# Two heads' stick-breaking scores made together on the halves of the matmul array

## Chip, cores and metric

One core of one Trainium2 chip. The metric is the device time of the kernel in microseconds, the median of several executions.

## What is computed

Two transformer blocks one behind the other, at 512 tokens and width 1024, in fp32. The change is in the first block's stick-breaking attention, 8 heads of 64:

```python
z = einsum('bhqd,bhkd->bhqk', q, k) * scale            # scores
strict = key_idx < q_idx
log_one_minus = where(strict, log_sigmoid(-z), 0)
suffix = cumsum(log_one_minus, reverse=True) - log_one_minus
w = where(strict, exp(log_sigmoid(z) + suffix), 0)
out = einsum('bhqk,bhkd->bhqd', w, v)
```

The query, key and value projections come before it; other projections of the same normalised input (latent ranks, gates) don't depend on it.

## The kernel before

The program is written engine by engine, with semaphores; each engine runs its own list in order. Weights come in chunks through three `raw` buffers; ScalarE copies a chunk into a rounded high part `whi`, VectorE subtracts it and gets `wlo`, each in four buffers. A projection tile is `project`: for 8 blocks of the inner dimension, three matmuls (low x high, high x low, high x high) of 512 columns into one PSUM bank, 24 in all. `bank(b)` waits until what was in bank b has been read (`free[b]`).

For the queries, ScalarE copies each head's 64 rows out of PSUM into a tile of its own (`qp[:, h, :]`), on rows 0 to 63 for even heads and 64 to 127 for odd ones; GpSimd fills the other 64 rows with zeros. Keys of two heads share a tile (`kp[:, h // 2, :]`). So a head's scores are a product over all 128 rows.

The attention of 8 heads is a loop over four pairs `pr`, with h = 2 pr. For one head:

- TensorE, `sb_qk`: transposed scores of four key blocks (512, 384, 128 and 256 query columns, the causal part only), each with a mask added by a small bf16 matmul. They lie in three banks, 0 to 2 for even heads and 3 to 5 for odd ones.
- VectorE, `sb_pre` (L1814): min(score, 40) into `sp`; ScalarE, `sb_pre` (L1313): exp, then ln(1 + x).
- VectorE, `sb_pre2` (L1822): maximum with the scores. ScalarE, `sb_pre2` (L1320): rounded copy `sph`; before it writes, it waits for SBSUF(h - 1), the suffix matmuls of the head before, which read the same single buffer. Low part `spl` by VectorE (last 256 columns, also in `sb_pre2`, waiting for the rounded copy) and by GpSimd (`sb_low`, 896 columns).
- TensorE, `sb_suffix`: suffix sums as products with triangular and all-ones tiles, added onto the scores. ScalarE, `sb_weights`: exp into `sp`.
- TensorE, `sb_pv`, once a pair: product with the values, head h into rows 0 to 63 of bank 6 and head h+1 into rows 64 to 127. VectorE copies it out (OA, L1846).

Between these steps every engine calls `next(fa)`, its share of one "filler": on TensorE a `project` (cq, ckv, kr, sz, mz, ga in turn) into bank 7 (three of the ga tiles go elsewhere), on ScalarE the conversion of a coming chunk, on VectorE the low part of that chunk, in some of the early fillers also a reduction over a chunk of `w_ada` (L1684), and then the copy of the filler's result out of its bank. The fillers are called equally often on all three engines, but in each engine's own order. Before the change, of one pair:

```
TensorE  sb_qk(h+1) | F1 | sb_suffix(h) | F2 | sb_qk(h+2) | F3 | sb_suffix(h+1) | F4 | sb_pv | F5
ScalarE  F1 | weights(h) | pre(h+1) | F2 | pre2(h+1) | F3 | weights(h+1) | F4 | pre(h+2) | F5 | pre2(h+2)
VectorE  F1 | pre(h+1) | F2 | pre2(h+1) | F3 | F4 | OA | pre(h+2) | F5 | pre2(h+2)
```

Ahead of the loop stand TensorE sb_qk(0), F0; ScalarE and VectorE pre(0), pre2(0), F0. In pair 2 ScalarE has eight silu activations between F5 and pre2.

Of the kernel before, what the change touches and what calls it, by code (L numbers as in the profile page):

```python
# [11 lines left out]
ALU = mybir.AluOpType  # L12
# [3 lines left out]
S = 512  # L16
# [86 lines left out]
BK = [0, 1, 2, 1]  # L103
# [3 lines left out]
KB_ORDER = (0, 1, 3, 2)  # L107
# [64 lines left out]
def build(nc, w_all, cst_d, rc_d, gc_d, rm_d, vec_d, x_d, c_d, pos_d, ada_d, p_d, out_d):  # L172
# [13 lines left out]
    with top:  # L186
# [3 lines left out]
        def sig(n, keys=(0,), step=1):  # L190
            return Sig(sem(n), keys, step)

        def sb(stack, name, shape, dt=F32):
            return stack.enter_context(nc.sbuf_tensor(name, shape, dt))

        PB = [top.enter_context(nc.psum_tensor(f"pb{i}", [128, 512], F32)) for i in range(8)]
# [23 lines left out]
        zs = sb(one, "zs", [128, 8, S])  # L220
# [15 lines left out]
            rn = sb(pre, "rn", [128, S])  # L236
            rk = sb(pre, "rk", [128, S])
        with ExitStack() as s1:
            qp = sb(s1, "qp", [128, 8, S])
            kp = sb(s1, "kp", [128, 4, S])  # L240
            sbv = sb(s1, "sbv", [128, 4, S])
            sp = sb(s1, "sp", [128, 2, 1280])
            sph = sb(s1, "sph", [128, 1280], F32R)
            spl = sb(s1, "spl", [128, 1280], F32R)
# [64 lines left out]
        identB, mcB, msB, mgB = (bcst[:, i, :] for i in range(4))  # L309
# [41 lines left out]
        def sb_out(h, kb):  # L351
            return PB[3 * (h % 2) + BK[kb]][:, BO[kb]:BO[kb] + LEN[kb]]
# [38 lines left out]
        MODS = sig("dve_mods", range(NB))  # L391
        ZPLE = sig("act_zple", range(8))

        QZERO = sig("pool_qzero", (0, 1))
        QPE, KPE, SBV = sig("act_qp", range(8)), sig("dve_kp", range(4)), sig("act_sbv", range(4))
        SBQK, SBMIN, SBLN, SBMAX, SBHI, SBLO0, SBLO1, SBSUF = (
            sig(n, range(8)) for n in ("pe_sbqk", "dve_sbmin", "act_sbln", "dve_sbmax", "act_sbhi", "pool_sblo",
                                       "dve_sblo", "pe_sbsuf"))
# [42 lines left out]
        def proj(name, idx=0, q=0):  # L441
            return PROJ((name, idx, q))
# [58 lines left out]
        def pool_program(e):  # L501
            G = Queue(e)
# [7 lines left out]
                e.tensor_tensor(dst, buf[64:96, 0, :], buf[64:96, 1, :], ALU.add).then_inc(ROPED.sem, 1)  # L510

            def sb_low(h):
                G.wait_ge(*QZERO(1))
                G.wait_ge(*SBHI(h))
                if h > 1:
                    G.wait_ge(*ROPED("kr"))
                if h:
                    G.wait_ge(*SBSUF(h - 1))
                e.tensor_tensor(spl[:, 0:896], sp[:, h % 2, 0:896], fr(sph[:, 0:896]), ALU.subtract).then_inc(SBLO0.sem, 1)
# [26 lines left out]
            G.wait_ge(*GPS.tick())  # L546
            e.tensor_scalar(ang[:, :], ang[:, :], lim, -lim, ALU.min, ALU.max).then_inc(ANG.sem, 1)

            G.wait_ge(*ROPE())
            G.wait_ge(*proj("pp", 1, 3))  # L550
            for r in range(2):
                if r:
                    G.wait_ge(*QZERO(0))
                e.memset(qp[64 - 64 * r:128 - 64 * r, :, :].rearrange("p (m r) n -> p m r n", r=2)[:, :, r, :], 0.0
                         ).then_inc(QZERO.sem, 1)
            for h in range(8):
                sb_low(h)
                if h == 1:
# [41 lines left out]
        def tensor_program(e):  # L600
            T = Queue(e)
            free = [[] for _ in range(8)]

            def mm(out, lhs, rhs, start, stop):
                return e.matmul(out, lhs, rhs, start=start, stop=stop, skip_group_check=True)  # L605

            def bank(b):

                for s, v in free[b]:
                    T.wait_ge(s, v)  # L610
# [98 lines left out]

            project_group([("sbq", i, 128, i) for i in range(4)], h1)  # L710
            for m in range(4):
                free[m] = [QPE(2 * m + 1)]
            for m in range(4):
                project("sbk", m, 128, 4 + m, h1)
                free[4 + m] = [KPE(m)]
# [30 lines left out]
                    free[b] = [GA67(m)]  # L746
                yield

            def sb_qk(h):
                T.wait_ge(*QPE(h))  # L750
                T.wait_ge(*QZERO(h % 2))
                T.wait_ge(*KPE(h // 2))
                T.wait_ge(*CONST())
                for kb in KB_ORDER:
                    out = sb_out(h, kb)
                    bank(3 * (h % 2) + BK[kb])
                    mm(out, kp[:, h // 2, 128 * kb:128 * kb + 128], qp[:, h, 128 * kb:512], kb != 3, False)
                    t = mm(out[:, 0:128], identB, msB, False, False)
                t.then_inc(SBQK.sem, 1)

            def sb_suffix(h):
                i = h % 2
                T.wait_ge(*SBMAX(h))
                for kb in range(4):
                    mm(sb_out(h, kb)[:, 128 * (3 - kb):128 * (4 - kb)], cb(O_TRI if kb == 3 else O_NONES),
                       sp[:, i, 896:1024], False, False)
                T.wait_ge(*SBLO0(h))
                T.wait_ge(*SBLO1(h))
                for kb in range(3):
                    for jb in range(kb, 3):  # L770
                        o = 128 * (jb - kb)
                        for src in (sph, spl):
                            t = mm(sb_out(h, kb)[:, o:o + LEN[jb]], triR if jb == kb else nonesR,
                                   src[:, SO[jb]:SO[jb] + LEN[jb]], False, False)
                t.then_inc(SBSUF.sem, 1)
                for b in range(3):
                    free[3 * i + b] = [SBW((h, b))]
# [15 lines left out]
            next(fa)  # L793
            for pr in range(4):
                h = 2 * pr
                sb_qk(h + 1)
                next(fa)
                sb_suffix(h)
                next(fa)
                if pr < 3:  # L800
                    sb_qk(h + 2)
                next(fa)
                sb_suffix(h + 1)
                next(fa)
                sb_pv(pr)
                if pr < 3:
                    next(fa)
            next(fa)

# [385 lines left out]
        def scalar_program(e):  # L1195
# [3 lines left out]
            def copy(out, in_, **kw):  # L1199
                return e.activation(out, in_, ACT.Copy, **kw)  # L1200
# [67 lines left out]
            A.wait_ge(*TRIG("cos"))  # L1268
            for m in range(4):
                A.wait_ge(*proj("sbq", m))  # L1270
                for r in range(2):
                    copy(qp[64 * r:64 * r + 64, 2 * m + r, :], PB[m][64 * r:64 * r + 64, :], scale=0.125
                         ).then_inc(QPE.sem, 1)
            for m in range(4):
                conv("sbk", m)
            for c in range(4):
# [36 lines left out]
            def sb_pre(h):  # L1313
                x = sp[:, h % 2, :]
                A.wait_ge(*SBMIN(h))
                e.activation(x, x, ACT.Exp).then_inc(ACS.sem, 1)
                A.wait_ge(*ACS.tick())
                e.activation(x, x, ACT.Ln, bias=one_c).then_inc(SBLN.sem, 1)

            def sb_pre2(h):  # L1320
                A.wait_ge(*SBMAX(h))
                if h:
                    A.wait_ge(*SBSUF(h - 1))
                copy(sph[:, :], sp[:, h % 2, :]).then_inc(SBHI.sem, 1)
# [7 lines left out]

            fa = filler_a()
            sb_pre(0)
            sb_pre2(0)
            next(fa)
            for pr in range(4):
                h = 2 * pr
                next(fa)
                sb_weights(h)  # L1340
                sb_pre(h + 1)
                next(fa)
                sb_pre2(h + 1)
                next(fa)
                sb_weights(h + 1)
                next(fa)
                if pr < 3:
                    sb_pre(h + 2)
                    next(fa)
                    if pr == 2:  # L1350
                        e.preload_act_table_set(SILU)
                        for m in range(8):
                            A.wait_ge(*ZE(m))
                            e.activation(zs[:, m, :], zs[:, m, :], ACT.Silu).then_inc(SIL.sem, 1)
                        e.preload_act_table_set(EXPLN)
                    sb_pre2(h + 2)
            next(fa)

            A.wait_ge(*ZA(3))
# [308 lines left out]
        def vector_program(e):  # L1668
# [3 lines left out]
            def tt(out, a, b, op):  # L1672
                return e.tensor_tensor(out, a, b, op)  # L1673
# [140 lines left out]
            def sb_pre(h):  # L1814
                V.wait_ge(*SBQK(h))
                if h > 1:
                    V.wait_ge(*SBPV(h // 2 - 1))
                for b, n in THIRDS:
                    t = e.tensor_scalar(sp[:, h % 2, 512 * b:512 * b + n], PB[3 * (h % 2) + b][:, 0:n], 40.0, None, ALU.min)
                t.then_inc(SBMIN.sem, 1)  # L1820
# [11 lines left out]

            fa = filler_a()
            sb_pre(0)
            sb_pre2(0)
            next(fa)
            for pr in range(4):
                h = 2 * pr
                next(fa)
                sb_pre(h + 1)  # L1840
                next(fa)
                sb_pre2(h + 1)
                next(fa)
                next(fa)
                V.wait_ge(*SBPV(pr))
                e.tensor_copy(qp[:, h, :], PB[6][:, :]).then_inc(OA.sem, 1)  # L1846
                if pr < 3:
                    sb_pre(h + 2)
                    next(fa)
                    sb_pre2(h + 2)  # L1850
            for m in range(4):
                V.wait_ge(*SIL(m))
                V.wait_ge(*OA(m))
                tt(zs[:, m, :], zs[:, m, :], qp[:, 2 * m, :], ALU.mult).then_inc(ZA.sem, 1)
            next(fa)

            for k in range(5):
# [553 lines left out]
```

## Time and profile before

| | |
|---|---|
| median of 3 runs | 1385.64 us (1383.92 to 1389.07) |
| profiled execution, its time | 1384.75 us |
| its span | 1382.9 us |
| busy: PE, weight loads, DVE, ACT, POOL | 1283.2, 1004.9, 704.0, 499.5, 101.1 us |
| chain that ended last: PE, DVE, ACT | 76%, 13%, 7% |

PE is TensorE's matmuls, PEld its weight loads, DVE VectorE, ACT ScalarE, POOL GpSimd. A row of the timeline gives the start in us from the span's start, the length, engine, line, operation, tiles written and read, shape and count; a bracket gives the idle time of that engine before it and what ended it. L605 is the matmul helper, which all of TensorE's projections and scores go through. Ends of matmuls are modelled: from one start to the next is the better measure. An fp32 matmul of the program stands as two passes.

### The profile page before, as it was taken

The page shows a single profiled execution, that of the slowest core. Times are in us where ns is not written, and L with a number is a line of the kernel's source. Part 1 is how long each engine was busy: PE and PEld are TensorE (multiplying, and loading weights), DVE is VectorE, ACT ScalarE, POOL GpSimd, SP SyncE. Part 2 cuts the span into 40 slices and gives each one's busy share as a digit, 9 for nine tenths or more (in the row PEclk, how much of TensorE's full clock was granted, in tenths as well). Part 3 has the DMA queues.
Part 4 walks back from the last instruction along what each step waited for, and adds up shares of the span by engine and source line. Part 5 has one row for each costly group of instructions (what it writes and reads, how often), then busy time and mean ns, then how long its engine had stood idle before and what let it go on. Part 6 is the DMA issues. An engine that isn't in the chain of part 4 may idle for free.

```text
span 1382.9 us, 14956 instructions
## 1 busy us (share of the span) xinstructions
PE 1283.2 (93%) x6048; PEld 1004.9 (73%) x6048; DVE 704.0 (51%) x1070; ACT 499.5 (36%) x793; POOL 101.1 (7%) x81
## 2 busy tenths in 40 slices
PE   2799999999998998999999898898999999999985
PEld 1577767776775776777776798786888888888864
DVE  3852574467556566536765675445333333332346
ACT  3451443443534343324456302223322222221233
POOL 7310111013000000000000300100000000000000
PEclk8799999999999999999999999999999999999998
DMA  7722332122121332221112000021322232333212
GB/s 283 274 77 76 103 122 77 62 69 88 46 61 46 97 128 94 84 84 61 46 51 72 16 1 1 31 75 51 118 92 91 94 102 94 114 110 100 93 48 85
DMA packets 35222, 118.16 MB, mean 85 GB/s; under 512 B 4001, under 2 KB 4257, under 8 KB 35153
## 3 DMA queue, kind: packets, MB, share of 16 engines
q1 hardware_dynamic: 33824, 112.68, 24.6%
q0 software_dynamic: 1328, 4.52, 1.1%
q8 instruction: 48, 0.79, 0.2%
q14 instruction: 22, 0.17, 0.0%
HBM read 112.99 MB, written 4.19 MB: 85 GB/s over the span
## 4 chain that ended last, share of the span: by engine, by line
PE 76%; DVE 13%; ACT 7%; issue 3%; DMA 1%; POOL 1%; DVEq 0%; SPq 0%; ACTq 0%
PE pb L605 73%; DVE wlo L1673 2%; DVE junk L1684 1%; ACT whi L1200 1%; DVE gq L1676 1%; PE pb L703 1%; ACT fP L1389 1%; DVE xT L1673 1%; PE pb L860 1%; DMA xT<-x_d 1%; DVE fP L1892 1%; DVE hlo L1673 1%; ACT mP L1389 1%; PE pb L687 1%; DVE mnm L1896 0%
## 5 line engine op out<-in xcount | busy, mean ns | idle before, releaser
L605 PE MATMUL pb<-hhi,wlo 128*128 128x512 f32 x1048 | 418.2, 399 | 17.6 <-ACT hhi L1200 9.8
L605 PE MATMUL pb<-hhi,whi 128*128 128x512 f32 x1048 | 417.2, 398 | 0.0
L605 PE MATMUL pb<-hlo,whi 128*128 128x512 f32 x1048 | 404.6, 403 | 11.9 <-DVE xT L1676 3.6
L1673 DVE TENSOR_TENSOR wlo<-raw,whi 128x1024 fp32r<-128x1024 f32 (+1 forms) x178 | 222.5, 1258 | 226.0 <-ACT whi L1200 225.8
L605 PEld LDWEIGHTS pb<-hhi,wlo 128*128 128x128 f32 x1048 | 198.1, 189 | 70.8 <-ACT hhi L1200 12.8
L605 PEld LDWEIGHTS pb<-hlo,whi 128*128 128x128 f32 x1048 | 198.8, 190 | 65.9 <-DVE wlo L1673 10.9
L605 PEld LDWEIGHTS pb<-hhi,whi 128*128 128x128 f32 x1048 | 198.4, 189 | 47.3
L1200 ACT ACTIVATE whi<-raw 128x1024 fp32r<-128x1024 f32 (+1 forms) x178 | 181.2, 1034 | 85.2 <-PE pb L605 85.1
L605 PE MATMUL pb<-alo,whi 128*128 128x512 f32 x176 | 69.6, 396 | 0.0
L605 PE MATMUL pb<-ahi,wlo 128*128 128x512 f32 x176 | 69.6, 396 | 0.0
L605 PE MATMUL pb<-ahi,whi 128*128 128x512 f32 x176 | 69.6, 395 | 0.0
L1200 ACT ACTIVATE ahi<-tmpf 128x512 fp32r<-128x512 f32 x22 | 13.9, 632 | 99.3 <-DVE tmpf L1673 99.3
L1673 DVE TENSOR_TENSOR tmpf<-tmpf,pb 128x512 f32<-128x512 f32 x22 | 15.1, 686 | 57.4 <-PE pb L605 57.4
L1605 ACT ACTIVATE sq<-xT 128x512 f32<-128x512 f32 x21 | 13.3, 632 | 84.8 <-DVE xT L1673 84.8
L1673 DVE TENSOR_TENSOR xT<-xT,pb 128x512 f32<-128x512 f32 x16 | 10.9, 686 | 55.2 <-PE pb L605 55.2
L605 PEld LDWEIGHTS pb<-ahi,wlo 128*128 128x128 f32 x176 | 33.1, 188 | 8.0
L605 PEld LDWEIGHTS pb<-ahi,whi 128*128 128x128 f32 x176 | 33.1, 188 | 8.0
L605 PEld LDWEIGHTS pb<-alo,whi 128*128 128x128 f32 x176 | 33.1, 188 | 8.0
L1632 ACT ACTIVATE tmpf<-pb 128x512 f32<-128x512 f32 x22 | 13.2, 599 | 61.9 <-PE pb L605 61.9
L1673 DVE TENSOR_TENSOR ssq<-ssq,sq 128x512 f32<-128x512 f32 x35 | 23.6, 691 | 21.7 <-ACT sq L1605 13.6
L1673 DVE TENSOR_TENSOR hlo<-tmpf,hhi 128x512 fp32r<-128x512 f32 x32 | 22.1, 691 | 21.5 <-ACT hhi L1200 21.5
L1200 ACT ACTIVATE hhi<-tmpf 128x512 fp32r<-128x512 f32 x32 | 20.2, 631 | 34.1 <-DVE tmpf L1676 33.9
(321 smaller groups left out, 1722.6 us busy)
## 6 DMA issues: line engine op xcount, KB each, us to landing
raw<-w_all SPq DMA_DIRECT2D x173, 512.0 KB, 3.5
adab<-ada_d SPq DMA_DIRECT2D x16, 512.0 KB, 9.2
raw<-w_all SPq DMA_DIRECT2D x10, 384.0 KB, 3.0
xT<-x_d SPq DMA_DIRECT2D x8, 256.0 KB, 8.6
ple_scratch<-zs SPq DMA_DIRECT2D x8, 256.0 KB, 2.3
xT<-x_d POOLq DMA_DIRECT2D x8, 256.0 KB, 3.0
out_d<-xT SPq DMA_DIRECT2D x8, 256.0 KB, 2.3
plr<-ple_scratch POOLq DMA_DIRECT2D x4, 256.0 KB, 3.6
```

What stands on the lines that cost most here:

```text
L605: return e.matmul(out, lhs, rhs, start=start, stop=stop, skip_group_check=True)
L687: t = e.matmul(PB[b][:, :], ones, src, start=True, stop=more is None)
L703: e.matmul(PB[7][:, :], ones, sq[:, b % 2, :], start=b == 0, stop=b == 7).then_inc(XSS.sem, 1)
L860: t = e.transpose(PB[b][:, o + 128 * (qi - kb):o + 128 * (qi - kb) + 128], P[:, PO[qi] + 128 * kb:PO[qi] + 128 * kb + 128], ident)
L1200: return e.activation(out, in_, ACT.Copy, **kw)
L1389: t = e.activation(d, src, ACT.Exp, bias=nm[:, i, qi:qi + 1], accum_out=rs[:, i, qi:qi + 1])
L1605: e.activation((sq[:, 1 - m % 2, :]) if m else ssq[:, :], xT[:, m, :], ACT.Square).then_inc(SQ.sem, 1)
L1632: e.activation(tmpf[:, j % 2, :], PB[2 * (j % 4)][:, :], ACT.Silu).then_inc(SG.sem, 1)
L1673: return e.tensor_tensor(out, a, b, op)
L1676: return e.scalar_tensor_tensor(out, a, s, b, op0, op1)
L1684: e.tensor_tensor_reduce(out=junk[:, :], in0=w, in1=cbt[:, :], scale=1.0, scalar=0.0, op0=ALU.mult, op1=ALU.add, accum_out=mod[:, at:at + ...
L1892: t = e.tensor_tensor_reduce(out=P[:, PO[qi]:PO[qi] + QN[qi]], in0=src, in1=cbt2[:, i, 0:QN[qi]], scale=1.0, scalar=-3.0e38, op0=ALU.add, ...
```

## The change

- `qp` has one tile for two heads: ScalarE copies all 128 rows at once. The zero fills on GpSimd and their waits are gone.
- `sb_qk(pr)` makes the scores of both heads of a pair: for each key block a matmul on rows 0 to 63 for head h and one on rows 64 to 127 for head h+1, in different banks; then the masks of head h, and those of head h+1.
- The orders of the three engines change with it:

```
TensorE  F1 | sb_suffix(h) | F2 | sb_suffix(h+1) | F3 | F4 | sb_pv | sb_qk(pair + 1) | F5
ScalarE  pre2(h+1) | F1 | weights(h) | F2 | weights(h+1) | F3 | F4 | pre(h+2) | pre(h+3) | pre2(h+2) | F5
VectorE  pre2(h+1) | F1 | F2 | F3 | F4 | OA | pre(h+2) | pre(h+3) | pre2(h+2) | F5
```

Ahead of the loop: TensorE sb_qk(pair 0), F0; ScalarE and VectorE pre(0), pre(1), pre2(0), F0. The silu block comes after F5 of pair 2.

```diff
-            qp = sb(s1, "qp", [128, 8, S])
+            qp = sb(s1, "qp", [128, 4, S])
...
-            G.wait_ge(*ROPE())
-            G.wait_ge(*proj("pp", 1, 3))
-            for r in range(2):
-                if r:
-                    G.wait_ge(*QZERO(0))
-                e.memset(qp[64 - 64 * r:128 - 64 * r, :, :].rearrange("p (m r) n -> p m r n", r=2)[:, :, r, :], 0.0
-                         ).then_inc(QZERO.sem, 1)
...
-            def sb_qk(h):
-                T.wait_ge(*QPE(h))
-                T.wait_ge(*QZERO(h % 2))
-                T.wait_ge(*KPE(h // 2))
+            def sb_qk(pr):
+
+                T.wait_ge(*QPE(pr))
+                T.wait_ge(*KPE(pr))
                 T.wait_ge(*CONST())
                 for kb in KB_ORDER:
-                    out = sb_out(h, kb)
-                    bank(3 * (h % 2) + BK[kb])
-                    mm(out, kp[:, h // 2, 128 * kb:128 * kb + 128], qp[:, h, 128 * kb:512], kb != 3, False)
-                    t = mm(out[:, 0:128], identB, msB, False, False)
-                t.then_inc(SBQK.sem, 1)
+                    for r in range(2):
+                        bank(3 * r + BK[kb])
+                        rows = slice(64 * r, 64 * r + 64)
+                        mm(sb_out(r, kb), kp[rows, pr, 128 * kb:128 * kb + 128], qp[rows, pr, 128 * kb:512], kb != 3, False)
+                for r in range(2):
+                    for kb in KB_ORDER:
+                        t = mm(sb_out(r, kb)[:, 0:128], identB, msB, False, False)
+                    t.then_inc(SBQK.sem, 1)
...
             for pr in range(4):
                 h = 2 * pr
-                sb_qk(h + 1)
                 next(fa)
                 sb_suffix(h)
                 next(fa)
-                if pr < 3:
-                    sb_qk(h + 2)
+                sb_suffix(h + 1)
                 next(fa)
-                sb_suffix(h + 1)
                 next(fa)
                 sb_pv(pr)
                 if pr < 3:
+                    sb_qk(pr + 1)
                     next(fa)
...
             sb_pre(0)
+            sb_pre(1)
             sb_pre2(0)
             next(fa)
             for pr in range(4):
                 h = 2 * pr
-                next(fa)
-                sb_pre(h + 1)
-                next(fa)
                 sb_pre2(h + 1)
                 next(fa)
                 next(fa)
+                next(fa)
+                next(fa)
                 V.wait_ge(*SBPV(pr))
-                e.tensor_copy(qp[:, h, :], PB[6][:, :]).then_inc(OA.sem, 1)
+                e.tensor_copy(qp[:, pr, :], PB[6][:, :]).then_inc(OA.sem, 1)
                 if pr < 3:
                     sb_pre(h + 2)
+                    sb_pre(h + 3)
+                    sb_pre2(h + 2)
                     next(fa)
-                    sb_pre2(h + 2)
```

## Rows read from the trace of the kernel before

**Rows 1.** The page, busy time of each engine (share of the span) and instructions
```profile
PE 1283.2 (93%) x6048; PEld 1004.9 (73%) x6048; DVE 704.0 (51%) x1070; ACT 499.5 (36%) x793; POOL 101.1 (7%) x81
```

**Rows 2.** Windows, pair end to pair end: busy PE, PEld, DVE, ACT, POOL; clock; DMA
```profile
178.09:221.70 43.61, 42.26 (x205) 31.71 (x203) 26.67 (x38) 17.45 (x20) 6.04 (x3) 1.00 0.36 121
...
262.93:303.70 40.77, 39.11 (x191) 30.54 (x189) 19.44 (x25) 23.75 (x29) 4.66 (x2) 1.00 0.17 55
sum 173.74, PE 167.39 PEld 127.90 DVE 93.43 ACT 77.64 POOL 20.03; mean PE 41.85 PEld 31.98 DVE 23.36 ACT 19.41 POOL 5.01
```

**Rows 3.** Timeline of PE, every row of the stage with a gap before it
```profile
144.21 0.47 PE L605 MATMUL pb<-hlo,whi 128*128 128x512 f32 x1 [3.34 <-DVE gbt L1784]
...
197.06 0.47 PE L605 MATMUL pb<-hlo,whi 128*128 128x512 f32 x1 [1.35 <-DVE zs L1803]
...
279.55 0.50 PE L605 MATMUL pb<-sph,rcst 128*128 128x512 f32 x1 [1.66 <-POOL spl L519]
```

**Rows 4.** Timeline of PE: scores of head 0, the filler behind them, next scores
```profile
129.96 1.02 PE L605 MATMUL pb<-qp,kp 128*128 128x512 f32 x2
...
130.82 0.22 PE L605 MATMUL pb<-bcst 128*128 128x128 bf16 x1
...
132.48 0.48 PE L605 MATMUL pb<-hlo,whi 128*128 128x512 f32 x1
...
138.16 1.02 PE L605 MATMUL pb<-qp,kp 128*128 128x512 f32 x2
```

**Rows 5.** Timeline of PE: values of pair 0 and the filler behind them
```profile
175.78 2.37 PE L605 MATMUL pb<-sp,sbv 128*64 128x512 f32 x16
178.09 0.48 PE L605 MATMUL pb<-hlo,whi 128*96 128x512 f32 x1
```

**Rows 6.** Timeline of DVE: chain of head 0 and the filler's copy
```profile
132.71 1.62 DVE L1819 TENSOR_SCALAR sp<-pb 128x512 f32<-128x512 f32 x3 [15.51 <-PE pb L605]
137.06 1.62 DVE L1673 TENSOR_TENSOR sp<-pb,sp 128x512 f32<-128x512 f32 x3 [2.74 <-ACT sp L1318]
...
140.97 2.49 DVE L1673 TENSOR_TENSOR wlo<-raw,whi 128x1024 fp32r<-128x1024 f32 x1 [0.52 <-ACT whi L1200]
143.38 0.68 DVE L1784 COPY gbt<-pb 128x512 f32<-128x512 f32 x1
```

**Rows 7.** Timeline of ACT: the same chain, second half
```profile
135.67 1.37 ACT L1318 ACTIVATE sp<-sp,epsc 128x1280 f32<-128x1280 f32 x1
138.72 1.27 ACT L1200 ACTIVATE sph<-sp 128x1280 fp32r<-128x1280 f32 x1 [1.69 <-DVE sp L1673]
139.90 1.04 ACT L1200 ACTIVATE whi<-raw 128x1024 fp32r<-128x1024 f32 x1
```

**Rows 8.** Timeline of DVE, pair 0: low part of head 1 to the next copy
```profile
163.90 0.42 DVE L1673 TENSOR_TENSOR spl<-sp,sph 128x256 fp32r<-128x256 f32 x1 [1.34 <-ACT sph L1200]
...
168.46 0.68 DVE L1784 COPY gbt<-pb 128x512 f32<-128x512 f32 x1
```

**Rows 9.** Timeline of DVE, pair 1: low part to the copy of sz0
```profile
190.40 0.43 DVE L1673 TENSOR_TENSOR spl<-sp,sph 128x256 fp32r<-128x256 f32 x1 [1.34 <-ACT sph L1200]
...
196.24 0.68 DVE L1803 COPY zs<-pb 128x512 f32<-128x512 f32 x1
```

**Rows 10.** Timeline of DVE, pair 2: low part to the next copy
```profile
232.41 0.42 DVE L1673 TENSOR_TENSOR spl<-sp,sph 128x256 fp32r<-128x256 f32 x1 [1.34 <-ACT sph L1200]
...
235.82 0.68 DVE L1803 COPY zs<-pb 128x512 f32<-128x512 f32 x1
```

**Rows 11.** A gap of a later stage, and windows (columns as rows 2) after gaps
```profile
431.39 0.50 PE L605 MATMUL pb<-hlo,whi 128*128 128x512 f32 x1 [3.27 <-DVE xT L1676]
144.20:148.00 3.80, 3.79 (x16) 3.09 (x17) 2.22 (x3) 1.48 (x2) 0.00 (x0) 1.00 0.76 219
431.40:435.00 3.60, 3.60 (x11) 2.90 (x12) 2.34 (x4) 0.64 (x1) 0.00 (x0) 0.70 0.55 148
435.00:439.00 4.00, 4.00 (x22) 2.79 (x20) 1.77 (x3) 0.60 (x1) 0.00 (x0) 0.84 0.00 0
```

More of the change, by code:

```diff
@@ L392, in build @@
         ZPLE = sig("act_zple", range(8))
-        QZERO = sig("pool_qzero", (0, 1))
-        QPE, KPE, SBV = sig("act_qp", range(8)), sig("dve_kp", range(4)), sig("act_sbv", range(4))
+        QPE, KPE, SBV = sig("act_qp", range(4)), sig("dve_kp", range(4)), sig("act_sbv", range(4))
         SBQK, SBMIN, SBLN, SBMAX, SBHI, SBLO0, SBLO1, SBSUF = (
@@ L512, in sb_low @@
             def sb_low(h):
-                G.wait_ge(*QZERO(1))
                 G.wait_ge(*SBHI(h))
@@ L711, in tensor_program @@
             for m in range(4):
-                free[m] = [QPE(2 * m + 1)]
+                free[m] = [QPE(m)]
             for m in range(4):
@@ L1270, in scalar_program @@
                 A.wait_ge(*proj("sbq", m))
-                for r in range(2):
-                    copy(qp[64 * r:64 * r + 64, 2 * m + r, :], PB[m][64 * r:64 * r + 64, :], scale=0.125
-                         ).then_inc(QPE.sem, 1)
+                copy(qp[:, m, :], PB[m][:, :], scale=0.125).then_inc(QPE.sem, 1)
             for m in range(4):
@@ L1338, in scalar_program @@
                 h = 2 * pr
+                sb_pre2(h + 1)
                 next(fa)
                 sb_weights(h)
-                sb_pre(h + 1)
-                next(fa)
-                sb_pre2(h + 1)
                 next(fa)
@@ L1834, in vector_program @@
             sb_pre(0)
+            sb_pre(1)
             sb_pre2(0)
@@ L1838, in vector_program @@
                 h = 2 * pr
-                next(fa)
-                sb_pre(h + 1)
-                next(fa)
                 sb_pre2(h + 1)
@@ L1844, in vector_program @@
                 next(fa)
+                next(fa)
+                next(fa)
                 V.wait_ge(*SBPV(pr))
-                e.tensor_copy(qp[:, h, :], PB[6][:, :]).then_inc(OA.sem, 1)
+                e.tensor_copy(qp[:, pr, :], PB[6][:, :]).then_inc(OA.sem, 1)
                 if pr < 3:
                     sb_pre(h + 2)
+                    sb_pre(h + 3)
+                    sb_pre2(h + 2)
                     next(fa)
-                    sb_pre2(h + 2)
             for m in range(4):
@@ L1853, in vector_program @@
                 V.wait_ge(*OA(m))
-                tt(zs[:, m, :], zs[:, m, :], qp[:, 2 * m, :], ALU.mult).then_inc(ZA.sem, 1)
+                tt(zs[:, m, :], zs[:, m, :], qp[:, m, :], ALU.mult).then_inc(ZA.sem, 1)
             next(fa)
```

## The prediction, made before the changed kernel ran

> **What bounds the kernel now.** I read the page's busy times first [rows 1]: the matmul engine (PE) is busy 93% of the span, the vector engine (DVE) half, the scalar engine (ACT) a third. Then the stretches from one head pair's end to the next [rows 2]: in the 174 us of the stick-breaking stage PE is busy 167.4 us at granted clock 1.00, i.e. at 2.4 GHz. Then its gaps there, by what ended them: 3.34, 1.35 and 1.66 us [rows 3], 6.35 us in all. So here every microsecond of PE work, and every microsecond that PE waits, moves the end. Its work is split: attention matmuls, and 21 "fillers" (a projection tile of 24 matmuls each, nearly all into bank 7) that cover the chain of DVE, ACT and GpSimd between scores and suffix sums. What the change does to that cover matters as much as the matmuls it saves.
>
> The first gap shows the mechanism. PE issued scores of head 0, one filler, scores of head 1, and then waited for a DVE copy of the filler's result out of bank 7. In DVE's order that copy stands behind both parts of head 0's chain.
>
> **The scores themselves.** One head's scores run from 129.96 to 132.48, 2.52 us [rows 4]: eight passes over 2 x 1280 columns and four masks. The 512-column pair of passes holds PE 0.86 us (129.96 to the mask at 130.82), so the columns alone are worth about 2.13 us and masks with weight loads 0.4. Two heads cost 5.04 us. The change puts head 0 on rows 0 to 63 and head 1 on rows 64 to 127. No row of before uses half the rows of the array. The nearest is the product with the values, where two heads stand on 64 output columns each: twice the columns of one head's scores, in 178.09 - 175.78 = 2.31 us [rows 5]. One behind the other they would be 4.27 us, so column halves run together. I take the same for row halves: 2.13 us, about 0.3 for loads that don't hide behind the short passes (twice the weight columns of that product), 0.6 for eight masks in a row, 0.1 for the change of mode: 3.1 us a pair. The bounds are 2.5 (the masks at 0.05 us each) and 5.04 (no overlap). Four pairs: 4 x (3.1 - 5.04) = -7.8 us.
>
> The Trainium skill speaks against the change in one place here (TensorEngine Tiling (Array Packing), Key Properties): changing the tiling mode drains the array. The trace's two switches a pair for the value product cost little, 2.31 us against 2.13 of columns and 0.1 us ahead of it; by the page alone I could put no number on it.
>
> **Stall A, ahead of the filler that follows a pair's first filler.** In the new DVE order, the lower clamp of both heads, then the maximum and low part of head h, stand ahead of the first filler's conversion and copy. Timed from the start of the scores: head h's last mask is finished at 3.0 (before, 132.71 - 129.96 = 2.75, with 2.52 on PE). From there the rows of DVE and ACT give the chain [rows 6, 7]: clamp from 132.71, exponential and logarithm to 137.04, maximum to 138.68, high part from 138.72 to 139.99, then ACT's weight split and DVE's low split (2.49 us, GpSimd busy beside it), the copy to 144.06. That is 11.35 us. New in it: ACT now does exponential and logarithm of head h+1 as well before the high part of h: it is done with them 2.6 us after 137.0, at 139.6 instead of a start at 138.72, so +0.85. The copy ends at 3.0 + 11.35 + 0.85 = 15.2, PE starts again 0.15 later, at 15.35 (144.21 against 144.06). Scores and one filler (132.48 to 138.16, less rounding 5.6 us at 0.233 a matmul) are over at 3.1 + 5.6 = 8.7. Stall A is 6.65 us. In the old order only pair 0 was built so; for the others the scores were made long ahead and the filler's copy stood between clamp and maximum. Now it comes four times: 26.6 us. (In pair 1 the filler is the rotary key, with one more weight reduction on DVE but GpSimd's low part moved behind the rotary sum: I take it as equal.)
>
> **Stall B, behind suffix(h).** DVE now does the maximum and low part of head h+1 ahead of filler F1's copy. The low part needs the high part, and ACT may write it only when suffix(h) is over, since both heads share one buffer; PE does suffix(h) *after* F1. So F2, right behind suffix(h), finds bank 7 full. What follows suffix(h) is: 0.23 us until its end is seen (as 132.71 against 132.48), 1.27 high part, 0.04, then DVE from the low part to the end of F1's copy, 0.15 to restart. The middle term stands in the trace for each pair: 163.90 to 169.14 = 5.24 (with a weight reduction on DVE in it) [rows 8]; 190.40 to 196.92 = 6.52 (normalising the latents) [rows 9]; 232.41 to 236.50 = 4.09, for the last two [rows 10]. B is 6.9, 8.2, 5.8, 5.8: 26.7 us. Before, F2's copy stood ahead of the maximum of head h+1, so that no copy waited for what follows suffix(h).
>
> **Given back.** The old gaps of 6.35 us go, being parts of A and B (the last also since the silu block now stands after the high part of head 6). In pair 1 the sum of squares of the latents, about 0.9 us of PE, falls into stall A. Fewer copies on ACT and no GpSimd fills of the zero halves: they lie under the sbk and sbv projections, DVE sat idle for 15.5 us before the first clamp [rows 6], so nothing. The rest of the kernel starts from the same state and shifts as one block.
>
> Sum: -7.8 + 26.6 + 26.7 - 6.35 - 0.9 = +38.2 us.
>
> **The clock.** Eight gaps of 5.6 to 8 us appear where the longest of the stage was 3.3. After the gap of 3.27 us that ended at 431.39 the granted clock was 0.70 and 0.84 over the next 3.6 and 4.0 us, that is partly at 1.2 GHz, a loss of 1.08 + 0.64 = 1.7 us; after the gap that ended at 144.21 it stayed at 1.00 [rows 11]. So a gap of 3.3 costs 0 or 1.7. Longer ones should be caught nearly always, but part of the slow stretch can fall in the gap: I take 1.4 each, +11 us; the bounds are 0 and 13.6. The Trainium skill (TensorE: Matmul & The Clock Gate, HAM oscillation) has a rule in the same direction, that pauses between bursts of matmuls bring the array back to half clock; by it alone none of the eight would be spared, which the 144.21 row shows is not so for 3.3 us.
>
> The profiled execution took 1384.75 us with a span of 1382.9, 0.9 under the median of 1385.64. 1384.75 + 38.2 + 11 = 1434; the difference to the median is less than the rounding. A change within 0.5% (7 us) could not be told from none.
>
> **The rivals.**
> *No overlap of the row halves.* For it: nothing of before uses them. Against: the column halves overlap [rows 5]. Scores then take 5.2 instead of 3.1, each pair's filler and chain start 2.1 us later, +8.4: 1442 us.
> *The clock stays up.* For it: 144.21. Then 1384.75 + 38.2 = 1423.
> *Only A or only B stalls*, for instance because high part and low part don't hold the copy as I read the queues: then 1384.75 - 7.8 + 26.6 - 6.35 + 4 x 1.4 = 1403.
> *Faster: the fillers' copies are not late.* Then the scores' saving is all there is: 1384.75 - 7.8 = 1377, and with the old gaps gone 1371. It decides by one number: the copy of a pair's first filler must end within 5.6 us of the scores' end. The chain's own row needs 11.35 us from the mask [rows 6, 7], and 3.34 us of stall [rows 3] were left even with 2.5 us of scores as more cover.
>
> **How the numbers follow.** Forecast (both stalls, overlap, clock lost in most gaps) 0.67; no overlap 0.12; clock stays up 0.12; one stall only 0.06; faster 0.03. The time is the forecast's, 1434 us. Its own bounds are 1426 to 1438; the range takes in the clock that stays and the row halves that don't overlap: 1419 to 1443, which leaves out about 2 in 10 with errors inside the chains. Faster 0.03, same 0.01, slower 0.96.
>
> **What would show it.** In the profile after: scores of a pair near 3.1 us and passes in two row groups whose spans lie over each other (5 if not); eight gaps of PE on L605 released by DVE copies (gbt, zs, xT), four of some 6.6 after one filler and four of 5.6 to 8 behind the suffix matmuls; PE busy in the stage down by some 8 us plus what the low clock adds; granted clock under 1.00 in each pair; a pair's period 51 to 54 us where it was 41 to 44. The prediction is wrong if DVE's copy comes within a filler's time of the scores, or if the gaps are there and something later takes up the delay.

## The result, and the profile after

The changed kernel takes 1438.62 us (median of 4 runs, 1436.5 to 1439.55) against 1384.78 us for the kernel before on the same chip: ratio 1.0379, 95% interval 1.0357 to 1.0401. It is 53.8 us slower; 1434 was predicted. On a second chip the ratio was 1.0397 (1.0382 to 1.0413). The profiled execution has a span of 1437.7 us, 54.8 more than before, and the clock of the whole execution fell from 0.981 to 0.959.

TensorE is busy for a smaller share of a longer span (the page, answering to [rows 1]):

```profile
span 1437.7 us, 14950 instructions
...
PE 1294.8 (90%) x6048; PEld 1015.3 (71%) x6048; DVE 702.8 (49%) x1070; ACT 496.2 (35%) x789; POOL 97.0 (7%) x79
```

The stage as in [rows 2], cut a little otherwise: from the first scores to pair 0's value product, and from there to the next pair's (columns: length, busy PE, PEld, DVE, ACT, POOL, granted clock, DMA share, GB/s):

```profile
129.55:185.24 55.69, 42.51 (x187) 33.25 (x187) 26.59 (x36) 20.52 (x27) 4.62 (x2) 0.88 0.20 65
185.24:243.77 58.53, 43.87 (x203) 32.93 (x202) 26.06 (x38) 17.82 (x21) 5.72 (x3) 0.88 0.28 99
243.77:300.58 56.81, 43.91 (x202) 33.85 (x201) 19.59 (x25) 14.93 (x17) 4.62 (x2) 0.88 0.14 47
300.58:357.14 56.56, 44.54 (x202) 34.59 (x201) 19.59 (x25) 22.70 (x28) 4.62 (x2) 0.88 0.13 40
sum 227.59, PE 174.84 PEld 134.62 DVE 91.84 ACT 75.96 POOL 19.59; mean PE 43.71 PEld 33.66 DVE 22.96 ACT 18.99 POOL 4.90
```

Cut in the same way the stage before took 301.39 - 129.96 = 171.4 us. All of the loss, 56.2 us, is here; the rest of the kernel moved as a block, within 1.4 us. Two things are to be seen: 52.8 us in which PE does nothing (227.59 - 174.84), and a granted clock of 0.88 where it was 1.00.

TensorE's timeline, the rows of one pair's scores (as [rows 4]):

```profile
187.54 2.43 PE L596 MATMUL pb<-qp,kp 64*128 64x512 f32 x16
189.91 0.62 PE L596 MATMUL pb<-bcst 128*128 128x128 bf16 x8
190.34 0.45 PE L596 MATMUL pb<-hlo,whi 128*96 128x512 f32 x1
```

Sixteen passes on 64 rows in 2.37 us, eight masks in 0.43: 2.80 us for two heads that took 5.04. So the row halves do run beside each other. (Pair 0's took 3.54 us, from 129.55 to 133.09, with 0.7 us of a wait in it, told below.) And its gaps, the first pair's two and the second's three (as [rows 3]):

```profile
145.36 0.77 PE L596 MATMUL pb<-hlo,whi 128*128 128x512 f32 x1 [6.43 <-DVE gbt L1775]
162.57 0.77 PE L596 MATMUL pb<-hlo,whi 128*128 128x512 f32 x1 [6.73 <-DVE gbt L1775]
202.75 0.77 PE L596 MATMUL pb<-hlo,whi 128*128 128x512 f32 x1 [5.78 <-DVE tmpf L1664]
221.54 0.77 PE L596 MATMUL pb<-hlo,whi 128*128 128x512 f32 x1 [8.00 <-DVE zs L1794]
238.00 0.47 PE L596 MATMUL pb<-hlo,whi 128*128 128x512 f32 x1 [0.88 <-DVE zs L1794]
```

Every one is a filler that waits for VectorE to read the filler before it out of bank 7 (a copy; at 202.75 the rotation of the rotary key). Pairs 2 and 3 have 6.43 and 5.59 each, pair 2 also 0.88.

VectorE and ScalarE ahead of the first gap's end (timelines, as [rows 6, 7]):

```profile
133.10 3.15 DVE L1810 TENSOR_SCALAR sp<-pb 128x512 f32<-128x512 f32 x6 [16.40 <-PE pb L596]
137.46 1.62 DVE L1664 TENSOR_TENSOR sp<-pb,sp 128x512 f32<-128x512 f32 x3 [1.22 <-ACT sp L1308]
141.18 0.42 DVE L1664 TENSOR_TENSOR spl<-sp,sph 128x256 fp32r<-128x256 f32 x1 [2.10 <-ACT sph L1192]
142.12 2.49 DVE L1664 TENSOR_TENSOR wlo<-raw,whi 128x1024 fp32r<-128x1024 f32 x1 [0.52 <-ACT whi L1192]
144.54 0.68 DVE L1775 COPY gbt<-pb 128x512 f32<-128x512 f32 x1
```
```profile
137.33 1.26 ACT L1306 ACTIVATE sp<-sp 128x1280 f32<-128x1280 f32 x1
138.62 1.36 ACT L1308 ACTIVATE sp<-sp,epsc 128x1280 f32<-128x1280 f32 x1
139.89 1.25 ACT L1192 ACTIVATE sph<-sp 128x1280 fp32r<-128x1280 f32 x1
```

The filler's copy, whose data was ready at 138.9 (the gap's start), starts at 144.54. In ScalarE's list exponential and logarithm of head h+1 stand ahead of the high part of head h: its maximum is done at 139.08, and the high part starts at 139.89, when that logarithm is through.

### The profile page after: what moved, and what is told of

The parts are those of the page before. It is cut to its first block, busy times and chain, and to the rows that moved or that the text cites. A ratio compares the mean times of both kernels' runs of the same rounds, so it can differ in the third digit from the quotient of the medians.

```text
span 1437.7 us, 14950 instructions
## 1 busy us (share of the span) xinstructions
PE 1294.8 (90%) x6048; PEld 1015.3 (71%) x6048; DVE 702.8 (49%) x1070; ACT 496.2 (35%) x789; POOL 97.0 (7%) x79
## 4 chain that ended last, share of the span: by engine, by line
PE 76%; DVE 13%; ACT 7%; issue 3%; DMA 1%; POOL 0%; DVEq 0%; SPq 0%; ACTq 0%
PE pb L596 74%; DVE wlo L1664 3%; DVE junk L1675 1%; ACT whi L1192 1%; DVE gq L1667 1%; PE pb L852 1%; PE pb L694 1%; ACT sp L1306 1%; DVE xT L1664 1%; ACT sp L1308 1%; PE pb L678 1%; DVE hlo L1664 1%; DMA xT<-x_d 1%; ACT mP L1380 1%; DVE mnm L1888 0%
## 5 line engine op out<-in xcount | busy, mean ns | idle before, releaser
L596 PE MATMUL pb<-hlo,whi 128*128 128x512 f32 x1048 | 411.2, 409 | 59.4 <-DVE zs L1794 21.8
L596 PE MATMUL pb<-hhi,wlo 128*128 128x512 f32 x1048 | 425.7, 406 | 16.3 <-ACT hhi L1192 9.0
L596 PE MATMUL pb<-hhi,whi 128*128 128x512 f32 x1048 | 424.2, 405 | 0.0
L596 PEld LDWEIGHTS pb<-hlo,whi 128*128 128x128 f32 x1048 | 203.2, 194 | 116.2 <-DVE wlo L1664 52.7
L596 PEld LDWEIGHTS pb<-hhi,wlo 128*128 128x128 f32 x1048 | 203.6, 194 | 70.8 <-ACT hhi L1192 12.7
L596 PEld LDWEIGHTS pb<-hhi,whi 128*128 128x128 f32 x1048 | 203.2, 194 | 48.5
L517 POOL TENSOR_TENSOR spl<-sp,sph 128x896 fp32r<-128x896 f32 x8 | 18.3, 2285 | 224.7 <-ACT sph L1192 224.6
```

## The experiments

The runs are numbered e1 to e10. Each ratio is against the kernel before on the same chip; "stage" is the time from the first scores to the last pair's value product, in the profiled execution. With the changed kernel at 1.0379 and 1.0397, differences of 0.002 (3 us) are not read.

**Full rows in the new order (e1).** The scores go back to 128 rows and the zero halves; nothing else:

```diff
-                        mm(sb_out(r, kb), kp[rows, pr, 128 * kb:128 * kb + 128], qp[rows, pr, 128 * kb:512], kb != 3, False)
+                        mm(sb_out(r, kb), kp[:, pr, 128 * kb:128 * kb + 128], qp[:, 2 * pr + r, 128 * kb:512], kb != 3, False)
```

> The changed kernel with its new order of work, but each head's scores again over all 128 rows, with the zero halves (two heads' matmuls one after the other, masks behind them). Theory (the new order makes the loss, the row halves gain): the scores of a pair take about 5 us instead of 2.80, and all that follows in the pair starts 2.2 us later, so the stage is 9 us longer: 1447 us, with the same eight gaps on TensorE. Rival (the row halves make the loss, by changes of mode or by slow matmuls): back to the time of the kernel before, 1385 us.

1445.19 us, ratio 1.0453 (1.0435 to 1.0472). A pair's scores take 4.84 us (189.08 to 193.92), all eight gaps are there with the same lengths to 0.01 us. The order makes the loss, and the row halves take 8 to 10 us off it.

**Half rows in the old order (e2).** The other part alone: one head's scores at a time, as before, on its own 64 rows:

```diff
-                    mm(out, kp[:, h // 2, 128 * kb:128 * kb + 128], qp[:, h, 128 * kb:512], kb != 3, False)
+                    rows = slice(64 * (h % 2), 64 * (h % 2) + 64)
+                    mm(out, kp[rows, h // 2, 128 * kb:128 * kb + 128], qp[rows, h, 128 * kb:512], kb != 3, False)
```

> The kernel before, one head's scores at a time in the old order, but on the 64 rows that hold its queries (the zero rows are still made, and not read). Theory (a half alone gains nothing, only two beside each other do, and a change of rows costs next to nothing): 1385 us, within 3 us of the kernel before; a head's scores stay at 2.5 us. Rival (the use of halves costs by itself): each of eight score blocks longer by a microsecond or more, 1393 us or above.

1391.09 us, ratio 1.0058 (1.0038 to 1.0078): 8 us slower, which I had not expected. One head's scores in this run's timeline:

```profile
159.37 1.12 PE L605 MATMUL pb<-qp,kp 64*128 64x512 f32 x2
160.42 0.23 PE L605 MATMUL pb<-bcst 128*128 128x128 bf16 x1
160.58 0.91 PE L605 MATMUL pb<-qp,kp 64*128 64x384 f32 x2
161.42 0.23 PE L605 MATMUL pb<-bcst 128*128 128x128 bf16 x1
161.58 0.48 PE L605 MATMUL pb<-qp,kp 64*128 64x128 f32 x2
162.00 0.23 PE L605 MATMUL pb<-bcst 128*128 128x128 bf16 x1
162.16 0.70 PE L605 MATMUL pb<-qp,kp 64*128 64x256 f32 x2
162.79 0.23 PE L605 MATMUL pb<-bcst 128*128 128x128 bf16 x1
162.83 0.48 PE L605 MATMUL pb<-hlo,whi 128*128 128x512 f32 x1
```

3.46 us (159.37 to 162.83) where a head took 2.52: 0.94 us for eight changes between 64 and 128 rows, 0.12 us each on average. Both directions pay: a mask, on full rows as before, now takes 0.16 us to the next start instead of 0.05, and a product on a half 0.14 to 0.19 more than on all rows. Eight heads make 7.5 us. So the rival was right in kind: using halves costs, at each change of mode.

That this is nearly the whole loss is chance. With longer scores as cover the stage's gaps shrank from 6.35 to 3.27 us (-3.1), and three fillers ran partly at the low clock, 7.12, 7.23 and 7.22 us instead of 5.67 (+4.5). Two of the three had no gap ahead of them; here the scores and the start of the filler behind them:

```profile
204.89:208.35 3.46, 3.46 (x14) 1.50 (x13) 2.65 (x5) 0.77 (x1) 0.00 (x0) 1.00 0.46 150
208.35:212.00 3.65, 3.65 (x11) 2.89 (x11) 2.60 (x2) 2.39 (x3) 2.35 (x1) 0.53 0.00 1
```

So the granted clock can fall without a pause. All four executions of this run had a clock of 0.976 or 0.977 over the whole kernel, six of the seven of the kernel before on this chip 0.980 or 0.981. Whether it is the alternation with halves that brings the clock down, no run separates.

In the changed kernel all matmuls on halves stand together and the masks behind them, two changes a pair, and the cost is lost in the 2.80 us. The rule of the Trainium skill that changing the tiling mode drains the array (TensorEngine Tiling (Array Packing), Key Properties) agrees; here is its size for these shapes.

**F1's copy ahead of head h+1's maximum (e3).** One step moved on two engines, against the gap behind suffix(h):

```diff
 VectorE and ScalarE, at the top of a pair
-                sb_pre2(h + 1)
                 next(fa)
+                sb_pre2(h + 1)
```

> The changed kernel with one step moved on VectorE and ScalarE: maximum, high and low part of head h+1 stand behind the copy and conversion of filler F1 instead of ahead of it. Theory: the four gaps behind suffix(h) (6.73, 8.00, 5.59, 5.59 us, 25.9 in all) go, and with them the slow clock that followed them (F2 and the suffix start behind them took about 8.6 us over their 5.6 each): 1438.6 - 34.5 = 1404 us; the four gaps behind a pair's first filler stay at 5.8 to 6.4 us. Rival (the gaps are moved, not removed: the chain of head h+1 then holds up suffix(h+1)): gaps ahead of suffix(h+1) of several us, and a time of 1420 us or above.

1406.56 us, ratio 1.0166 (1.0144 to 1.0188): 29 to 32 us back of the 34 expected. Who waited for whom on PE in this run (total, times, longest):

```profile
PE pb L596 <- DVE zs L1794: 8.2, 3, 6.4
PE pb L596 <- DVE xT L1799: 6.4, 1, 6.4
PE pb L596 <- DVE gbt L1775: 6.4, 1, 6.4
PE pb L596 <- DVE tmpf L1664: 5.8, 1, 5.8
```

The four gaps behind suffix(h) are gone and no new one stands ahead of suffix(h+1); the other four are unchanged. (zs: one of 6.4 and two of 0.88.) The stage of the profiled execution, at 1402.26 us the fastest of the four, is 191.6 us, 36 less.

**The gaps filled with matmuls (e4).** 20 matmuls on data that nobody uses, ahead of F1 and behind suffix(h). They are extra work; nothing is left out:

```diff
+            def pad(n):
+                bank(6)
+                for _ in range(n):
+                    mm(PB[6][:, :], hhi[:, 0, 0:128], hhi[:, 0, :], True, True)
...
+                pad(20)
                 next(fa)
                 sb_suffix(h)
+                pad(20)
```

> The changed kernel with 20 more matmuls (512 columns, into bank 6, whose content is then overwritten) at each of the eight places at which TensorE waits: they take 4.7 us at full clock and lie in the gaps. They are work beyond the reference's, and nothing is left out. Theory (the gaps cost twice, by their length and by the slow clock behind them): the clock stays at its full level through the stage, the fillers behind the gaps go back from 7 to 8.4 us to 5.6, and about 17 us come back: 1421 us. Rival (the slow clock costs nothing of its own, since other engines set the pace there): 1438 us or more.

1425.09 us, ratio 1.0321 (1.0291 to 1.0351): with 160 matmuls *more*, 8 to 11 us faster than the changed kernel. The windows show why. First the changed kernel, first gap and its filler in two parts, then the second gap:

```profile
138.90:145.36 6.46, 0.03 (x1) 0.03 (x1) 3.84 (x5) 3.30 (x4) 2.31 (x1) 0.79 0.00 0
145.36:149.30 3.94, 3.94 (x9) 3.12 (x10) 1.38 (x3) 0.52 (x1) 0.00 (x0) 0.50 0.42 133
149.30:152.91 3.61, 3.61 (x16) 2.90 (x15) 0.00 (x0) 0.00 (x0) 0.00 (x0) 0.97 0.00 0
155.80:162.57 6.77, 0.04 (x1) 0.03 (x1) 5.18 (x5) 2.32 (x3) 2.31 (x1) 0.79 0.09 15
162.57:166.50 3.93, 3.92 (x9) 3.15 (x10) 3.02 (x4) 2.71 (x5) 0.00 (x0) 0.50 0.73 249
```

The granted clock falls to 1.2 GHz inside the gap and stays there for 3.9 us of the filler behind it. The same filler, and the one behind the second gap, in the run with the gaps filled, and then the one of pair 2:

```profile
144.55:150.22 5.67, 5.67 (x25) 4.59 (x25) 1.38 (x3) 0.52 (x1) 0.00 (x0) 1.00 0.30 92
159.94:165.61 5.67, 5.67 (x24) 4.60 (x25) 3.06 (x4) 2.72 (x5) 0.00 (x0) 1.00 0.77 261
...
253.33:260.56 7.23, 7.23 (x25) 5.72 (x26) 1.38 (x3) 0.00 (x0) 0.00 (x0) 0.76 0.22 73
```

A filler takes 5.67 us at full clock. The eight behind the changed kernel's gaps take 7.55, 7.50, 7.86, 7.07, 7.69, 8.08, 8.23 and 8.38, together 62.4: the slow clock costs 62.4 - 8 x 5.67 = 17.0 us. Not all came back: two fillers were still at 0.76, behind the last 1.94 us of their gaps, and in pair 1 the padding waited 2.0 us for bank 6 and then ran at 0.57 for 4 us. The three cost 4.6 us. The other remaining gaps, 1.10 to 2.23 us, had full clock behind them.

**Both copies first (e5).** The step of e3, and the same for the pair's first filler:

```diff
 VectorE                              ScalarE
                 sb_pre(h + 2)                        sb_pre(h + 2)
                 sb_pre(h + 3)       +                next(fa)
+                next(fa)                             sb_pre(h + 3)
                 sb_pre2(h + 2)                       sb_pre2(h + 2)
-                next(fa)            -                next(fa)
```

> Run e3 and the same for the other gap: VectorE converts and copies a pair's first filler ahead of the maximum and low part of head h, ScalarE does the same ahead of exponential and logarithm of head h+1. Theory: from the end of the scores the copy is then held up only by the weight split behind ScalarE's logarithm of head h (ends 7.3 us after the scores began, split 1.0, low part 1.2, copy 0.7: 10.3, where the filler ends at 8.4), so the four gaps fall from 6.4 to about 2 us and the clock stays up behind them: 1406 - 4 x 4.3 - 8 = 1381 us, at the level of the kernel before. Rival (the chain of head h, moved back, holds up suffix(h) by as much): new gaps ahead of suffix(h), and a time above 1392 us.

1387.48 us, ratio 1.0012 (0.9999 to 1.0025): back at the kernel before, 6 us short of the expectation. No gap of the rival's size stands ahead of suffix(h). The first gap of each pair is 1.44 to 1.54 us, five others are 0.8 to 1.5, and one of 4.04 us is new: the silu block of pair 2 now stands ahead of ScalarE's part of F1. The filler behind it took 8.29 us.

**Three fillers ahead of suffix(h) (e6, and e7 on full rows).** Another order: scores, F, F, F, suffix(h), F, suffix(h+1), F, values, with VectorE clamp, clamp, F, pre2(h), F, F, pre2(h+1), F, F. The second filler of pairs 0, 2 and 3 goes into bank 6, which is empty there.

```diff
 TensorE
             for pr in range(4):
                 h = 2 * pr
+                sb_qk(pr)
+                for _ in range(3):
+                    next(fa)
-                next(fa)
                 sb_suffix(h)
                 next(fa)
                 sb_suffix(h + 1)
                 next(fa)
-                next(fa)
                 sb_pv(pr)
-                if pr < 3:
-                    sb_qk(pr + 1)
-                    next(fa)
...
-                    project(*(("sz", m) if m < 4 else ("mz", m - 4)), 128, 7, h1)
+                    b = 6 if m == 5 else 7
+                    project(*(("sz", m) if m < 4 else ("mz", m - 4)), 128, b, h1)
```

> Paired scores on row halves with another order of work: a pair is scores, three fillers, suffix(h), a filler, suffix(h+1), a filler, values. VectorE: clamps, F, maximum and low part of h, F, F, maximum and low part of h+1, F, F. ScalarE accordingly, the silu block in the last pair. The second filler of pairs 0, 2 and 3 goes into bank 6, so that two fillers in a row don't share a bank. Theory: all eight gaps go but for 1 to 2.5 us in pairs 0 and 1, where the weights are converted only one chunk ahead, and the scores' 9 us (5.04 to 2.80 a pair) show at last: 1373 us, faster than the kernel before. Rival (the cover is the limit in any order): 1383 us or more.

> Run e6 with the scores over all 128 rows and the zero halves, as in run e1. Theory: 4 x 2.24 = 9 us slower than e6: 1382 us. Rival (the scores' saving is hidden by other engines even in this order): the time of e6.

On half rows 1383.11 us, ratio 0.9992 (0.9975 to 1.0009); on full rows 1389.57, ratio 1.0036 (1.0019 to 1.0053). They were expected at 1373 and 1382, and missed it by 10 and 8 us. In e6 there were gaps of 0.76 and 2.25 us (weights not split yet) in pair 0, 1.53 and 4.27 in pair 1, 2.27 in pair 3 (a filler in a bank that waited for head 6's weights), 11.1 us in all; two fillers behind them were partly at the low clock, 8.46 and 7.22 us instead of 5.67. Pair 2, without a gap, took 38.81 us where it was 41.24 before, and 40.87 in e7. So the scores' saving shows in this order, 2.06 us a pair, but the gaps take it back.

**The gaps mended (e8).** Weights are converted two chunks ahead in the first pairs too, the latents' sum of squares stands behind its neighbour filler, that filler of pair 3 goes to bank 7, and values are projected into banks 4 to 7, away from bank 3 that the scores need first. Beside it the same on full rows (e9), and the kernel *before* with the two mends that fit it (e10).

```diff
-            project_nat("sbv", [3, 4, 5, 6], h1)
+            project_nat("sbv", [4, 5, 6, 7], h1)
...
-                conv("kr")
+                conv("kr", 0, 4)
...
-                    b = 0 if m == 4 else 6 if m == 2 else 7
+                    b = 6 if m == 2 else 7
                     project("ga", m, 128, b, h1)
```

> Run e6 with what its gaps pointed to: weights converted two chunks ahead in the first pairs too, the sum of squares of the latents behind sz0 (bank 7, sz0 in bank 6), ga4 in bank 7 instead of a bank that waits for head 6's weights, values projected into banks 4 to 7. Theory: the clean pair of e6 took 38.8 us between values (41.2 before); with all four like it and two sums of squares the stage takes some 158 us instead of 171.4: 1372 us, ratio 0.990. Rival (other engines set the pace once TensorE has less to do): 1380 us or above.

> Run e8 with the scores over all 128 rows and the zero halves. Theory: the scores' saving is all that tells the two apart, 4 x (4.4 - 2.4) to 4 x 2.24 = 8 to 9 us: 1381 us. Rival: as e8.

> The kernel before, its order and its scores, with two of e8's mends: weights two chunks ahead in the first pairs, values projected into banks 4 to 7. It tells how much of e8 is the mends. Theory: the gap of 3.34 us comes from the chain of head 0 and stays, so at most 2 us: 1384 us. Rival (the mends are what makes e8 fast): 1376 us or less.

| | us | ratio, 95% interval | stage |
|---|---|---|---|
| new order mended, half rows | 1374.17 | 0.9933 (0.9914 to 0.9953) | 163.1 |
| the same, full rows | 1385.26 | 0.9999 (0.9986 to 1.0012) | 171.3 |
| old order, two mends | 1384.88 | 1.0001 (0.9985 to 1.0017) | 173.2 |

The first is faster than both kernels, by 9 us over the one before. A pair without a gap, half rows and then full rows:

```profile
209.69:248.50 38.81, 38.81 (x201) 30.61 (x200) 19.71 (x25) 15.06 (x17) 4.75 (x2) 1.00 0.20 68
```
```profile
212.35:253.21 40.86, 40.86 (x201) 32.04 (x200) 19.71 (x25) 15.06 (x17) 4.74 (x2) 1.00 0.20 66
```

PE is busy throughout in both, and the difference is the scores' 2.05 us. In the stage it makes 8.1 us, where 8 to 9 were expected. The medians are 11 us apart because the executions differ in their clock over the whole kernel: those at 0.979 to 0.981 took 1373.5 us in e8 (three) and 1381.4 in e9 (three), 8 us apart, and 1382.5 for the kernel before on this chip (five), 9 above e8. The clock also tells e10: its first gap is the 3.34 us of the kernel before, but the filler behind it took 7.20 us, not 5.67.

The 1372 us expected of e8 were nearly met, the stage's 158 were not (163.1). Three gaps are left in it: 1.60 us in pair 0 and 3.63 in pair 3, behind the copy of a filler (the second where ScalarE has the silu block), and 0.93 in pair 1 behind ScalarE's root of the latents' squares. The filler behind the 3.63 took 7.22 us.

## Why the prediction was right, point by point

The time lay in the range, and the sign and the mechanism were as forecast; the forecast's own bounds ended at 1438, 0.6 us below it. The terms of the sum, with what the profile after shows:

| step | predicted | measured |
|---|---|---|
| scores, 4 pairs | -7.8 | 4 x (2.80 - 5.04) = -9.0 |
| stall A | 26.6 | 6.43 + 5.78 + 6.43 + 6.43 = 25.1 |
| stall B | 26.7 | 6.73 + 8.00 + 5.59 + 5.59 = 25.9 |
| old gaps gone | -6.35 | -6.35 |
| sum of squares inside stall A | -0.9 | in the 5.78 already |
| slow clock | 11 | 17.0 |
| not seen | | 2 x 0.88, and 0.7 in the first scores: 2.5 |
| sum | 49 | 55.1 (stage: 56.2, span: 54.8) |

Part of the agreement is luck: scores and stalls came out 2.6 us better than forecast, the clock and what was not seen 8.5 us worse.

*The scores.* Half rows overlap as column halves do: 2.37 us for the matmuls, and the masks 0.43 rather than 0.6. The full-row run shows it by itself: 4.4 us for the matmuls, masks as long.

*Stall A.* The chain was read off [rows 6, 7] and came as read: the clamp starts 3.55 us after the scores of pair 0 began (3.0 predicted; the scores were 2.80 plus 0.7 of a wait that I had not seen: head h+1's first bank, 3, was still being copied; in e8, with the values in banks 4 to 7, it is gone), and the copy ends 12.1 us behind that, 11.35 + 0.85 predicted. That the filler behind the rotary key could be taken as equal was nearly so, 5.78 and 1.0 of the sum of squares against 6.43.

*Stall B.* Predicted 6.9, 8.2, 5.8, 5.8; each was 0.2 less. e3 shows the cause: with the copy moved ahead, all four vanish and none appears elsewhere.

*The clock* is the term that was mis-sized: 2.1 us for each gap instead of 1.4. I had taken something off the 1.7 of [rows 11] because part of the slow stretch would fall in the gap. It does (0.79 in the gap), but the low stretch was longer as a whole. In the gap and its filler together the clock fell short of full by (1 - 0.79) x 6.43 + (1 - 0.73) x 7.55 = 3.4 us, and by 3.4 to 3.5 at each of the other seven, where it was 1.7 at [rows 11], all of it behind the gap. What is paid is the part that doesn't fall into the gap, so the longest gap cost least, 1.40 us, and the last one of 5.59 us most, 2.71 (gap, its filler; then the other two):

```profile
213.54:221.54 8.00, 0.00 (x1) 0.04 (x1) 5.79 (x8) 4.66 (x7) 2.32 (x1) 0.76 0.11 26
221.54:228.61 7.07, 7.07 (x25) 5.63 (x25) 2.21 (x3) 1.06 (x1) 0.00 (x0) 0.78 0.73 269
329.10:334.69 5.59, 0.00 (x1) 0.03 (x1) 3.67 (x4) 4.40 (x6) 2.31 (x1) 0.92 0.00 0
334.69:343.07 8.38, 8.38 (x24) 6.64 (x25) 0.99 (x1) 0.00 (x0) 0.00 (x0) 0.64 0.36 115
```

Filling the gaps with matmuls showed that this is a cost of its own. The Trainium skill's rule that pauses return the array to half clock (TensorE: Matmul & The Clock Gate, HAM oscillation) agrees with the trace for all eight. For shorter gaps the runs go both ways: full clock behind 3.34 us in the kernel before and not in e10, behind 2.26 in e7 and not behind 2.27 in e6.

*Not seen:* two fillers in a row through one bank cost a copy, 0.88 us (F3 and F4, pairs 1 and 2; in pair 0 a sum of squares of 1.04 us stands between them, in pair 3 one of them is in bank 0). The old order had scores, suffix or values between two fillers of bank 7.

*The signs.* Two were given wrongly. A pair's period was to be 51 to 54 us and was 58.53, 56.81 and 56.56 (values to values); the sum itself, 49 us over four pairs of 41 to 44, says 53 to 56. PE's busy time in the stage was to fall by 8 us plus what the low clock adds: it rose from 165.1 to 174.8, since the low clock adds about twice what the scores save.

*The rivals.* "No overlap" and "the clock stays up" are ruled out by the profile, "one stall only" is what e3 built, at 1406.6 against my 1403. "Faster" had one condition, that the copies are not late; the mended order meets it but for three gaps, 6.2 us in all, and is faster.

What isn't settled: how much of the mended kernel's gain is the order itself. Full rows in that order equal the kernel before in median and, to 0.2 us, in the stage (171.3 against 171.4); but e9's stage has 1.5 us of low clock in it, that of the kernel before none. I read only that the order alone gains nothing that can be told. Nor is it shown why a short gap, or none, is followed by the low clock in one place and not in another.

## What to carry to other kernels

When one engine's work is made shorter, look at what its length was covering: here 2.2 us of scores were saved a pair, and the order that came with it put the copies that free a bank behind a 12 us chain. In in-order queues put what frees a buffer for the busiest engine ahead of anything that waits for that engine. Count an idle gap of the matmul engine as more than its length, here 6 us and 2 more. Compare kernels that are a few us apart by a stage of the profile, or by executions of equal clock: here the medians gave 11 us for a change of 8.

## What the runs showed of the hardware

- Two fp32 products over 64 rows each, on the two row halves and into different banks, run beside each other: 2.37 us where one after the other took 4.4. It needs no interleaving finer than one product each.
- Going between 64 and 128 rows cost 0.12 us a change on average (e2). Alternating with small full-row matmuls made a head's scores 0.94 us longer, 7.5 us over eight heads, though no matmul had more columns than before.
- In e2 the granted clock fell to 1.2 GHz twice with no gap ahead, behind scores on halves that alternated with masks; why is open.
- A gap of 5.6 to 8 us cost 17.0 / 8 = 2.1 us of clock behind it on average (1.4 to 2.7, least behind the longest gap), and a kernel with 160 useless matmuls in its gaps was 8 to 11 us faster than the same without.
